# A fused encoder layer on Trainium2: residual rows folded into PSUM by identity products in the final stage

## The chip, the cores and the metric

The kernel is one program on one core of one Trainium2 chip. The metric is device time in microseconds for one execution, the median of several runs. All times inside the profile are microseconds from the start of the profiled execution's span.

## The reference, cut to what matters

One encoder layer over 1024 tokens of width 1024: RMSNorm, an input projection, three token mixers, an output projection with a residual add (its result is called `x1` in the kernel), then RMSNorm, a two-level router and a mixture of 32 experts of which each token uses two, a second residual add and a final RMSNorm.

```python
x = x + jnp.concatenate([o_a, o_b, o_c], axis=-1) @ w_out          # x1
x = x + hierarchical_moe(rmsnorm(x, norm2_g), ...)                  # two experts a token, each with its gate
...
return rmsnorm(x, final_g)                                          # x * rsqrt(mean(x*x) + eps) * final_g
```

What the final stage has to compute for each token is therefore: `s = x1 + gate0*y0 + gate1*y1`, where `y0` and `y1` are the output rows of its two experts, and then `s * rsqrt(mean(s*s) + 1e-6) * final_g`.

## The kernel before, in words

The stages run one after the other on one core: input projection, attention and pooling mixers, output projection, router, and then a loop over the 32 experts (from about 400 us to 806 us). In that loop every expert gathers its at most 80 rows from a table in HBM, TensorE multiplies them with the expert's weights, and the result rows are scattered by GpSimd's indirect DMA into the HBM tensor `expert_rows` (`y_d`): first choices in its rows 0 to 1023, second choices in rows 1024 to 2047. A branch for experts with more than 80 rows (`n_ovf > 0`) is in the program, and does no work on this input.

**The final stage**, which the change is about, works on 8 tiles of 128 tokens, `t = 0..7`; `x1[:, t, :]` (128 partitions x 1024 float32) already lies in SBUF.

- *SyncE* (lines 590 to 608) waits until all scatters have landed, and issues 16 loads of 512 KB each (`load_rows`, L596 and L597: `y0[t]`, then `y1[t]`, in the order of `t`), both on the semaphore `yc_in[t]`. After these it issues the 8 stores of the result (`store`, L601), each after a wait for `c_out`. All of them go into one hardware queue.
- *VectorE* makes, in the last expert's shadow, eight diagonal matrices `gdiag[i][k]` (L1627: the identity times the gate of each token). It then runs `add_rows(t)` and `finish(t)` in the order add 0, add 1, finish 0, add 2, finish 1 and so on to add 7, finish 6, finish 7.
- *TensorE* does a part of the sums. For the tiles in `PE_TILES = (1, 2, 4, 6)` it computes `gdiag0 @ y0 + gdiag1 @ y1` in two PSUM banks (L950, four float32 products of 128x128 by 128x512 a tile; the trace shows each as two records). `add_rows` of such a tile is one VectorE addition of PSUM and `x1` (L1650). For the other tiles (0, 3, 5, 7) `add_rows` is two multiply-adds from SBUF (L1655), no product.
- *ScalarE* takes the sum of squares of each finished sum (L1224) and adds eps (L1226), *GpSimd* raises it to the power -1/2 (L1848), and VectorE's `finish(t)` (L1661) multiplies the sum by that factor and by `final_g` into `fo[t]`. All three engines do this in the order of `t`.

The wait before TensorE's last-stage products is for both loads of a tile:

```python
for i, t in enumerate(PE_TILES):
    pe.wait_ge(diag_made, 2 * i + 2)
    pe.wait_ge(yc_in[t], 32)
```

Of the PSUM banks, `ps[0]` and `ps[1]` serve the expert loop's transposes, 2 and 3 its gate and up products, 4 to 7 its down products. The last expert's rows are copied out of banks 6 and 7 by ScalarE (L1207, counted in `y_out`) and VectorE (L1630, counted in `y_half`).

Of the kernel before, what the change touches and what calls it, by code (L numbers as in the profile page):

```python
# [24 lines left out]
ALU = mybir.AluOpType  # L25
ACT = mybir.ActivationFunctionType
# [6 lines left out]
P = 128  # L33
D = 1024
S = 1024
TT = S // P
# [26 lines left out]
POOL_LAG = 2  # L63
POOL_OPS = 16
PE_TILES = (1, 2, 4, 6)


ORDER = [4, 0, 5, 1, 11, 12, 13, 2, 3, 10, 6, 7, 8, 9]
# [41 lines left out]
def encoder(nc, x, norm1_g, w_in, nat_win, swa_sink, pool_w, pool_scale, w_out, norm2_g,  # L110
# [6 lines left out]
    y_d = nc.dram_tensor("expert_rows", [2 * S, D], F32).ap()  # L117

    with ExitStack() as ctx:
# [5 lines left out]
        def at(name, shape, dt, off):  # L125
            return nc.alloc_sbuf_tensor_at(name, shape, dt, offset=base + int(off))

        def sem(name):
            return ctx.enter_context(nc.semaphore(name))
# [3 lines left out]
        ident = at("ident", [P, P], F32, o); o += 512  # L133
        ones = at("ones", [P, P], F32, o); o += 512
        ut = at("ut", [P, P], F32, o); o += 512
        gbc = at("gbc", [P, D], F32, o); o += 4096
# [5 lines left out]
        stat = at("stat", [P, 4, TT], F32, o); o += 128  # L142
# [61 lines left out]
        x1 = at("x1", [P, TT, D], F32, TD)  # L204
# [42 lines left out]
        y0 = [at(f"y0{i}", [P, D], F32, H + 8192 * i) for i in range(TT)]  # L247
        y1 = [at(f"y1{i}", [P, D], F32, H + 8192 * i + 4096) for i in range(TT)]
        fo = [at(f"fo{i}", [P, D], F32, W + 4096 * i) for i in range(TT)]

        gdiag = [[at(f"gdiag{k}_{i}", [P, P], F32, W + 32 * KB + 512 * (2 * i + k)) for k in range(2)]
                 for i in range(len(PE_TILES))]

        ps = ctx.enter_context(nc.psum_tensor("ps", [P, 8, 512], F32))
# [107 lines left out]
        v_hT = sem("v_hT")  # L362
        v_ya = sem("v_ya")
        v_yv = sem("v_yv")
        yc_in = [sem(f"yc_in{i}") for i in range(TT)]
        c_sum = sem("c_sum")
        y_half = sem("y_half")
        diag_made = sem("diag_made")
        c_mm = sem("c_mm")
        c_eps = sem("c_eps")  # L370
        c_sq_done = sem("c_sq_done")
# [57 lines left out]

        def sums_done(t):  # L430

            return sum(1 if x in PE_TILES else 2 for x in range(t + 1))

        def raw_half(w, e, a):

# [20 lines left out]
        def _(sp):  # L456
# [136 lines left out]
            sp.wait_ge(y_put[0], n_ovf * 16 + 16 * (N_EXP // 2))  # L593

            def load_rows(t):
                sp.dma_start(y0[t][:], y_d[t * P:(t + 1) * P, :]).then_inc(yc_in[t], 16)  # L596
                sp.dma_start(y1[t][:], y_d[S + t * P:S + (t + 1) * P, :]).then_inc(yc_in[t], 16)  # L597

            def store(t):
                sp.wait_ge(c_out, t + 1)  # L600
# [2 lines left out]
            for t in range(TT):  # L603
                load_rows(t)
# [6 lines left out]
        def _(pe):  # L611
# [222 lines left out]
            def rows_transposed(src):  # L834

                for k in range(KT):
                    mm = nc.tensor.transpose(ps[:, k // 4, (k % 4) * COLS:(k % 4 + 1) * COLS],  # L837
                                             src[:, k * P:(k + 1) * P], ident[0:COLS, 0:COLS])
                return mm
# [71 lines left out]
            def v_gate_up(xTu):  # L911
                for f in range(4):
                    c0 = (f % 2) * P
                    for k in range(KT):
                        mm = nc.tensor.matmul(ps[:, 2, f * COLS:(f + 1) * COLS], wgu[0][:, f // 2, k, c0:c0 + P], xTu[:, k, :],
                                              start=(k == 0), stop=(k == KT - 1))
                return mm

            def v_down(hTu):
                for n in range(2):  # L920
                    for j in range(2):
                        mm = nc.tensor.matmul(ps[0:CAP, 4 + n, :], hTu[:, j, 0:CAP], wd[0][:, j, n * 512:(n + 1) * 512],
                                              start=(j == 0), stop=(j == 1))
                return mm
# [4 lines left out]
            with pe.If(n_ovf > 0):  # L929
                pe.wait_ge(v_hots, 1)  # L930
                for c in range(2 * TT):
                    mm = nc.tensor.matmul(ps[0:CAP, 3, 0:2 * N_OVF], ovf_row[:, c, :], ovf_tile[:, c].rearrange("p a j -> p (a j)"),
                                          start=(c == 0), stop=(c == 2 * TT - 1))
                mm.then_inc(v_list_mm, 1)
                with pe.Fori(0, N_OVF) as j:
                    with pe.If(j < n_ovf):
                        pe.wait_ge(v_x, j * 16 + 16)
                        rows_transposed(xg[0]).then_inc(v_tr, 1)
                        pe.wait_ge(v_xT, j + 1)
                        pe.wait_ge(v_w, j * 48 + 48)  # L940
                        v_gate_up(v_xTt).then_inc(v_gu, 1)
                        pe.wait_ge(v_hT, j + 1)
                        v_down(v_hTt).then_inc(down_done, 1)

            for i, t in enumerate(PE_TILES):
                pe.wait_ge(diag_made, 2 * i + 2)
                pe.wait_ge(yc_in[t], 32)
                for n in range(2):
                    for k, y in enumerate((y0[t], y1[t])):
                        mm = nc.tensor.matmul(ps[:, 2 * (i % 4) + n, :], gdiag[i][k][:], y[:, n * 512:(n + 1) * 512],  # L950
                                              start=(k == 0), stop=(k == 1))
                mm.then_inc(c_mm, 1)


        @block.scalar
        def _(act):
# [74 lines left out]
            def o_evacuate(s):  # L1031
                kind, i, g, _, _ = steps[s]
                oi = o_steps.index(s)
                act.wait_ge(pv_done, vnum[(s, last_chunk[s])] + 1)
                bank = ps[:, 6 + oi % 2, :]
                if kind == "na":
                    dst, src = oT[:, 0:2, i * P:(i + 1) * P], bank[:, 0:2 * P].rearrange("p (t q) -> p t q", t=2)
                else:
                    dst, src = oT[:, 2:6, i * P:(i + 1) * P], bank.rearrange("p (t q) -> p t q", t=4)
                nc.scalar.copy(dst, src).then_inc(o_out, 1)  # L1040
# [179 lines left out]
                        nc.scalar.copy(ysb[0][:, 0:512], ps[0:CAP, 4, :]).then_inc(v_ya, 1)  # L1220

            for t in range(TT):
                act.wait_ge(c_sum, sums_done(t))
                nc.scalar.activation(fo[t][:], x1[:, t, :], ACT.Square, scale=D ** -0.5, accum_out=stat[:, 0, t:t + 1]).then_inc(c_sq_done, 1)  # L1224
                act.wait_ge(c_sq_done, t + 1)
                nc.scalar.activation(stat[:, 1, t:t + 1], stat[:, 0, t:t + 1], ACT.Identity, bias=eps_col[:]).then_inc(c_eps, 1)  # L1226

# [2 lines left out]
        def _(dve):  # L1230
# [393 lines left out]
            dve.wait_ge(down_done, N_EXP - 1)  # L1624
            for i, t in enumerate(PE_TILES):
                for k in range(2):
# [16 lines left out]


            def add_rows(t):
                if t in PE_TILES:
                    i = PE_TILES.index(t)
                    dve.wait_ge(c_mm, i + 1)
                    b0 = 2 * (i % 4)
                    nc.vector.tensor_tensor(x1[:, t, :].rearrange("p (n d) -> p n d", n=2), ps[:, b0:b0 + 2, :],  # L1650
                                            x1[:, t, :].rearrange("p (n d) -> p n d", n=2), ALU.add).then_inc(c_sum, 1)
                    return
                dve.wait_ge(yc_in[t], 32)
                for k, y in enumerate((y0[t], y1[t])):
                    nc.vector.scalar_tensor_tensor(out=x1[:, t, :], in0=y[:], scalar=gates[:, k, t:t + 1], in1=x1[:, t, :],  # L1655
                                                   op0=ALU.mult, op1=ALU.add).then_inc(c_sum, 1)
                    dve.wait_ge(c_sum, sums_done(t) - 1 + k)

            def finish(t):
                dve.wait_ge(rstd_a, TT + t + 1)  # L1660
                nc.vector.scalar_tensor_tensor(out=fo[t][:], in0=x1[:, t, :], scalar=stat[:, 1, t:t + 1], in1=gbc[:],  # L1661
                                               op0=ALU.mult, op1=ALU.mult).then_inc(c_out, 1)

            dve.wait_ge(g_in, 48)
            add_rows(0)
            for t in range(TT):
                if t + 1 < TT:
                    add_rows(t + 1)
                finish(t)


        @block.gpsimd
# [238 lines left out]
```

## Time and profile before

| | us |
|---|---|
| median of 3 runs | 853.67 (852.27 to 855.41) |
| the profiled execution, its own time | 855.69 |
| span of that execution in the profile | 853.9 |
| TensorE busy | 749.4 (88%) |
| VectorE busy | 510.6 (60%) |
| ScalarE busy | 435.7 (51%) |
| GpSimd busy | 289.7 (34%) |
| last product of the expert loop ends | about 805.6 |
| from there to the end of the span | 48.3 |

The final stage is thus the last 5.7% of the span. The busy shares of the whole span say nothing of it: they are sums over stages with other limits. It has to be read from views that are limited to this stretch: the chain of waits, the timeline by engine, the landings of the DMAs and tables of windows. In a timeline row the columns are the start, the duration, engine, line, operation, tile written and tiles read, and in brackets the idle time of the engine before it with what ended it. PE is TensorE, PEld its weight loads, DVE VectorE, ACT ScalarE, POOL GpSimd, SPq SyncE's queue of DMA issues.

### The profile page before, as it was taken

How to read it: one execution, taken by the hardware profiler on the slowest of the kernel's cores; microseconds unless marked ns; L12 is line 12 of the kernel's file. 1: busy time of each engine (PE TensorE's matmuls, PEld its weight loads, DVE VectorE, ACT ScalarE, POOL GpSimd, SP SyncE). 2: the span in 40 equal slices, each digit the busy share in tenths (PEclk: the TensorE clock that was granted, in tenths of full speed). 3: DMA queues.
4: the chain of work that ended last, by engine and by line, in shares of the span. 5: the costliest groups of instructions: out<-in, count | busy, mean ns of one | idle time of the engine just before them, and what ended most of it. 6: DMA issues, size and time to landing. Idle time of an engine off the chain costs nothing.

```text
span 853.9 us, 10370 instructions
## 1 busy us (share of the span) xinstructions
PE 749.4 (88%) x3852; PEld 538.5 (63%) x3852; DVE 510.6 (60%) x776; ACT 435.7 (51%) x635; POOL 289.7 (34%) x240
## 2 busy tenths in 40 slices
PE   3899999999996888799899489999999999999761
PEld 2788888876664555488788456666666656656420
DVE  5551000016767888531357769888778888878547
ACT  6311112125555887700212278887777777778323
POOL 2533355615635767060101112222222233321111
PEclk9999999997999999999999589999999999999976
DMA  8362111100010000333463839999999999998195
GB/s 283 86 174 64 50 36 44 44 1 1 2 50 1 0 1 1 124 99 124 152 230 106 325 133 329 385 368 372 377 377 370 368 365 371 372 372 312 54 377 212
DMA packets 54947, 160.39 MB, mean 188 GB/s; under 512 B 9344, under 2 KB 24160, under 8 KB 46576
## 3 DMA queue, kind: packets, MB, share of 16 engines
q1 hardware_dynamic: 48352, 142.26, 46.1%
q0 software_dynamic: 6400, 16.92, 5.9%
q8 instruction: 32, 0.52, 0.2%
q10 hardware_dynamic: 144, 0.52, 0.2%
q14 instruction: 19, 0.16, 0.1%
HBM read 145.01 MB, written 18.87 MB: 192 GB/s over the span
## 4 chain that ended last, share of the span: by engine, by line
PE 60%; DMA 18%; DVE 10%; ACT 6%; issue 3%; SPq 1%; POOL 0%; POOLq 0%; ACTq 0%; DVEq 0%
DMA wgu<-in_expert_w_up 13%; PE ps L632 6%; PE ps L633 6%; PE ps L634 6%; PE ps L859 4%; PE ps L864 4%; PE ps L867 4%; PE ps L755 3%; PE ps L672 3%; PE ps L757 3%; PE ps L756 3%; PE ps L697 2%; DVE wgulo L1574 2%; PE ps L713 2%; PE ps L886 2%
## 5 line engine op out<-in xcount | busy, mean ns | idle before, releaser
L1574 DVE TENSOR_TENSOR wgulo<-wgu,unit 128x2048 fp32r<-128x2048 f32 x64 | 144.0, 2288 | 46.8 <-ACT unit L1137 46.8
L1137 ACT CAST unit<-wgu 128x2048 fp32r<-128x2048 f32 x64 | 120.3, 1909 | 33.1 <-DMA wgu<-in_expert_w_up 26.8
L1816 POOL DMA_INDIRECT expert_rows<-ysb,idx x32 | 51.8, 1618 | 169.4 <-ACT ysb L1184 160.1
L632 PE MATMUL ps<-hThi,whi 128*128 128x512 f32 x224 | 89.7, 400 | 4.2 <-DVE hTlo L1241 4.2
L633 PE MATMUL ps<-hTlo,whi 128*128 128x512 f32 x224 | 88.9, 397 | 0.0
L634 PE MATMUL ps<-hThi,wlo 128*128 128x512 f32 x224 | 88.7, 396 | 0.0
L1580 DVE TENSOR_TENSOR wdlo<-wd,unit 128x2048 fp32r<-128x2048 f32 x32 | 73.4, 2292 | 5.3 <-ACT unit L1146 5.3
L859 PE MATMUL ps<-unit,xThi 128*80 128x512 f32 x256 | 71.9, 402 | 0.0
L864 PE MATMUL ps<-unit,xTlo 128*80 128x512 f32 x256 | 70.0, 395 | 0.0
L867 PE MATMUL ps<-wgulo,xThi 128*80 128x512 f32 x256 | 69.8, 394 | 0.0
L1309 DVE CUSTOM_DVE_ANT_0 pna<-ps,te 128x512 f32<-128x512 f32 x16 | 10.9, 688 | 93.6 <-PE ps L672 93.4
L1771 POOL TENSOR_SCALAR pswa<-pswa,esum 128x384 f32<-128x384 f32 (+1 forms) x48 | 55.6, 1167 | 31.7 <-DVE esum L1329 31.2
L1809 POOL DMA_INDIRECT xg<-h_rows,idx x32 | 38.5, 1203 | 78.5 <-PE ps L837 63.7
L1146 ACT CAST unit<-wd 128x2048 fp32r<-128x2048 f32 x32 | 60.9, 1902 | 0.0
L755 PE MATMUL ps<-wohi,oThi 128*128 128x512 f32 x128 | 51.9, 405 | 4.0 <-DVE oTlo L1361 3.6
L864 PEld LDWEIGHTS ps<-unit,xTlo 128*80 128x80 f32 x256 | 38.2, 149 | 21.5 <-issue 0.7
L632 PEld LDWEIGHTS ps<-hThi,whi 128*128 128x128 f32 x224 | 43.0, 192 | 13.7 <-issue 4.7
L867 PEld LDWEIGHTS ps<-wgulo,xThi 128*80 128x80 f32 x256 | 38.2, 149 | 21.3 <-issue 0.7
L756 PE MATMUL ps<-wolo,oThi 128*128 128x512 f32 x128 | 50.1, 392 | 0.0
L757 PE MATMUL ps<-wohi,oTlo 128*128 128x512 f32 x128 | 50.1, 391 | 0.0
L1028 ACT ACTIVATE pswa<-pswa,mneg 128x385 f32<-128x385 f32 (+1 forms) x64 | 37.6, 589 | 22.5 <-DVE mneg L1322 22.1
L634 PEld LDWEIGHTS ps<-hThi,wlo 128*128 128x128 f32 x224 | 43.1, 193 | 9.3
(194 smaller groups left out, 1490.3 us busy)
## 6 DMA issues: line engine op xcount, KB each, us to landing
wgu<-in_expert_w_gate SPq DMA_DIRECT2D x32, 1024.0 KB, 17.4
wgu<-in_expert_w_up SPq DMA_DIRECT2D x32, 1024.0 KB, 21.9
wd<-in_expert_w_down SPq DMA_DIRECT2D x32, 1024.0 KB, 16.6
y<-expert_rows SPq DMA_DIRECT2D x16, 512.0 KB, 9.5
wraw<-in_w_in SPq DMA_DIRECT2D x14, 512.0 KB, 3.9
xin<-in_x SPq DMA_DIRECT2D x8, 512.0 KB, 5.6
xres<-in_x SPq DMA_DIRECT2D x16, 256.0 KB, 3.4
out<-fo SPq DMA_DIRECT2D x8, 512.0 KB, 2.6
```

Of the source, the lines that this page charges most:

```text
L632: nc.tensor.matmul(bank, whi[i % 2][:, k, :], hThi[:, k, cols], start=(k == 0), stop=False)
L633: nc.tensor.matmul(bank, whi[i % 2][:, k, :], hTlo[:, k, cols], start=False, stop=False)
L634: mm = nc.tensor.matmul(bank, wlo[i % 2][:, k, :], hThi[:, k, cols], start=False, stop=(k == KT - 1))
L755: nc.tensor.matmul(ps[:, g % 4, :], oThi[t][:, k, :], wohi[n][:, k, :], start=(k == 0), stop=False)
L756: nc.tensor.matmul(ps[:, g % 4, :], oThi[t][:, k, :], wolo[n][:, k, :], start=False, stop=False)
L757: mm = nc.tensor.matmul(ps[:, g % 4, :], oTlo[t][:, k, :], wohi[n][:, k, :], start=False, stop=(k == KT - 1))
L859: nc.tensor.matmul(bank, xThi[e % 2][:, 4 * a + k, :], hi[:, :, k * DE:(k + 1) * DE], start=(a == 0 and k == 0), stop=False)
L864: nc.tensor.matmul(bank, xTlo[e % 2][:, 4 * a + k, :], hi[:, :, k * DE:(k + 1) * DE], start=False, stop=False)
L867: mm = nc.tensor.matmul(bank, xThi[e % 2][:, 4 * a + k, :], lo[:, :, k * DE:(k + 1) * DE], start=False, stop=(a == 1 and k == 3))
L1137: nc.scalar.copy(weight_unit(e, a)[:], raw_half(wgu, e, a)).then_inc(ahi_done, 1)
L1574: nc.vector.tensor_tensor(raw_half(wgulo, e, a), raw_half(wgu, e, a), weight_unit(e, a)[:].bitcast(F32), ALU.subtract).then_inc(alo_done, 1)
L1580: nc.vector.tensor_tensor(wdlo[e % RING][:].rearrange("p j d -> p (j d)").rearrange("p (a f) -> p a f", a=2), wd[e % RING][:].rearrange("p ...
```

## The change

Nothing before the final stage changes. In it:

- TensorE first runs `FILL_LAST = 16` products of the identity with 128 columns of ones into bank 0, whose result is overwritten. It then puts the residual rows `x1[:, t, :]` of its four tiles into their banks by products with the identity (8 products of 128x128 by 128x512, `start=True`), before any row has landed. The expert rows are then accumulated on top (`start=False`), `y0` as soon as it is there and `y1` after it. Four tiles use all eight banks; the fourth waits for `y_half`, since VectorE copies the last expert's rows out of bank 7. 
- Inside the branch for overflow, which isn't taken here, TensorE gets two further waits.
- The addition in VectorE (L1650) is gone. For these four tiles ScalarE's sum of squares and VectorE's `finish` read PSUM directly (`sum_of(t)`), and ScalarE waits for TensorE's `c_mm` in place of VectorE's `c_sum`.
- Each load has a semaphore of its own (`yc_in[k][t]`), so that a multiply-add or product of `y0` does not wait for `y1`.
- VectorE's order is written out: add 0, finish 0, add 3, finish 1, 2, 3, add 5, finish 4, add 7, finish 5, 6, 7.

```diff
+FILL_LAST = 16
...
-        yc_in = [sem(f"yc_in{i}") for i in range(TT)]
+        yc_in = [[sem(f"yc_in{k}_{i}") for i in range(TT)] for k in range(2)]
...
         def sums_done(t):
 
-            return sum(1 if x in PE_TILES else 2 for x in range(t + 1))
+            return 2 * sum(x not in PE_TILES for x in range(t + 1))
+
+        def sum_of(t):
+
+            if t in PE_TILES:
+                i = PE_TILES.index(t)
+                return ps[:, 2 * i:2 * i + 2, :]
+            return x1[:, t, :].rearrange("p (n d) -> p n d", n=2)
...
             def load_rows(t):
-                sp.dma_start(y0[t][:], y_d[t * P:(t + 1) * P, :]).then_inc(yc_in[t], 16)
-                sp.dma_start(y1[t][:], y_d[S + t * P:S + (t + 1) * P, :]).then_inc(yc_in[t], 16)
+                sp.dma_start(y0[t][:], y_d[t * P:(t + 1) * P, :]).then_inc(yc_in[0][t], 16)
+                sp.dma_start(y1[t][:], y_d[S + t * P:S + (t + 1) * P, :]).then_inc(yc_in[1][t], 16)
...
                         v_down(v_hTt).then_inc(down_done, 1)
-
+                        pe.wait_ge(v_ya, j + 1)
+                        pe.wait_ge(v_yv, j + 1)
+
+            def last_rows(i, rows, weight, first, last):
+
+                for n in range(2):
+                    mm = nc.tensor.matmul(ps[:, 2 * i + n, :], weight[:], rows[:, n * 512:(n + 1) * 512], start=first, stop=last)
+                return mm
+
+            for _ in range(FILL_LAST):
+                nc.tensor.matmul(ps[:, 0, 0:P], ident[:], ones[:], start=True, stop=True)
             for i, t in enumerate(PE_TILES):
-                pe.wait_ge(diag_made, 2 * i + 2)
-                pe.wait_ge(yc_in[t], 32)
-                for n in range(2):
-                    for k, y in enumerate((y0[t], y1[t])):
-                        mm = nc.tensor.matmul(ps[:, 2 * (i % 4) + n, :], gdiag[i][k][:], y[:, n * 512:(n + 1) * 512],
-                                              start=(k == 0), stop=(k == 1))
-                mm.then_inc(c_mm, 1)
+                if i == 3:
+                    pe.wait_ge(y_half, 1)
+                last_rows(i, x1[:, t, :], ident, True, False)
+            pe.wait_ge(diag_made, 2 * len(PE_TILES))
+            for i, t in enumerate(PE_TILES):
+                pe.wait_ge(yc_in[0][t], 16)
+                last_rows(i, y0[t], gdiag[i][0], False, False)
+                pe.wait_ge(yc_in[1][t], 16)
+                last_rows(i, y1[t], gdiag[i][1], False, True).then_inc(c_mm, 1)
...
             for t in range(TT):
-                act.wait_ge(c_sum, sums_done(t))
-                nc.scalar.activation(fo[t][:], x1[:, t, :], ACT.Square, scale=D ** -0.5, accum_out=stat[:, 0, t:t + 1]).then_inc(c_sq_done, 1)
+                if t in PE_TILES:
+                    act.wait_ge(c_mm, PE_TILES.index(t) + 1)
+                else:
+                    act.wait_ge(c_sum, sums_done(t))
+                nc.scalar.activation(fo[t][:].rearrange("p (n d) -> p n d", n=2), sum_of(t), ACT.Square, scale=D ** -0.5,
+                                     accum_out=stat[:, 0, t:t + 1]).then_inc(c_sq_done, 1)
...
             def add_rows(t):
-                if t in PE_TILES:
-                    i = PE_TILES.index(t)
-                    dve.wait_ge(c_mm, i + 1)
-                    b0 = 2 * (i % 4)
-                    nc.vector.tensor_tensor(x1[:, t, :].rearrange("p (n d) -> p n d", n=2), ps[:, b0:b0 + 2, :],
-                                            x1[:, t, :].rearrange("p (n d) -> p n d", n=2), ALU.add).then_inc(c_sum, 1)
-                    return
-                dve.wait_ge(yc_in[t], 32)
+
                 for k, y in enumerate((y0[t], y1[t])):
+                    dve.wait_ge(yc_in[k][t], 16)
...
-                nc.vector.scalar_tensor_tensor(out=fo[t][:], in0=x1[:, t, :], scalar=stat[:, 1, t:t + 1], in1=gbc[:],
+                nc.vector.scalar_tensor_tensor(out=fo[t][:].rearrange("p (n d) -> p n d", n=2), in0=sum_of(t), scalar=stat[:, 1, t:t + 1],
+                                               in1=gbc[:].rearrange("p (n d) -> p n d", n=2),
                                                op0=ALU.mult, op1=ALU.mult).then_inc(c_out, 1)
...
             add_rows(0)
-            for t in range(TT):
-                if t + 1 < TT:
-                    add_rows(t + 1)
-                finish(t)
+            finish(0)
+            add_rows(3)
+            finish(1)
+            finish(2)
+            finish(3)
+            add_rows(5)
+            finish(4)
+            add_rows(7)
+            finish(5)
+            finish(6)
+            finish(7)
```

## Rows read from the trace of the kernel before

**Rows 1.** Chain that ended last, final stage: start, us, what.
```profile
807.14 3.73 DMA expert_rows<-ysb,idx
...
812.31 6.61 DMA y<-expert_rows
...
819.05 9.17 PE ps L950 x16
...
847.67 1.28 DVE fo L1661
```

**Rows 2.** Windows: stretch, length, busy PE, PEld, DVE, ACT, POOL, clock, DMA share, GB/s.
```profile
807.00:819.00 12.00, 0.00 (x0) 0.00 (x0) 2.57 (x2) 0.43 (x1) 0.91 (x1) 0.61 0.67 246
...
814.60:834.50 19.90, 15.23 (x30) 6.52 (x31) 11.18 (x10) 5.59 (x12) 2.33 (x3) 0.78 1.02 401
...
834.50:838.20 3.70, 1.02 (x3) 0.19 (x1) 3.67 (x4) 1.63 (x4) 1.53 (x2) 1.00 0.87 357
```

**Rows 3.** Timeline of VectorE in the final stage, three of its rows.
```profile
815.93 2.61 DVE L1655 SCALAR_TENSOR_TENSOR x<-y,gates,x 128x1024 f32<-128x1024 f32 x2 [9.64 <-DMA y<-expert_rows]
824.88 1.22 DVE L1650 TENSOR_TENSOR x<-ps,x 128x1024 f32<-128x1024 f32 x1 [6.34 <-PE ps L950]
...
842.90 2.60 DVE L1655 SCALAR_TENSOR_TENSOR x<-y,gates,x 128x1024 f32<-128x1024 f32 x2
```

**Rows 4.** Groups of instructions by line and shape: busy us, mean ns | idle before.
```profile
L1655 DVE SCALAR_TENSOR_TENSOR x<-y,gates,x 128x1024 f32<-128x1024 f32 x8 | 10.3, 1282 | 9.8 <-DMA y<-expert_rows 9.6
L1661 DVE SCALAR_TENSOR_TENSOR fo<-x,stat,gbc 128x1024 f32<-128x1024 f32 x8 | 10.2, 1280 | 1.0 <-POOL stat L1848 0.9
...
L1650 DVE TENSOR_TENSOR x<-ps,x 128x1024 f32<-128x1024 f32 x4 | 4.9, 1221 | 7.3 <-PE ps L950 7.3
```

**Rows 5.** SyncE's loads by line: issues, first and last start; then time to landing.
```profile
L596 SPq DMA_DIRECT2D y<-expert_rows x8: 335/443/870, 811.0 to 818.5; - x8
...
DMA to landing us min/median/max: 3.6/9.2/14.4
...
L597 SPq DMA_DIRECT2D y<-expert_rows x8: 432/441/894, 811.4 to 819.0; - x8
...
DMA to landing us min/median/max: 4.5/9.9/15.5
```

**Rows 6.** Stores 1, 3 and 8: issue, and under it its time to landing.
```profile
827.32 0.34 SPq L601 DMA_DIRECT2D out<-fo  x1
DMA to landing us min/median/max: 8.4/8.4/8.4
...
834.52 0.33 SPq L601 DMA_DIRECT2D out<-fo  x1
DMA to landing us min/median/max: 3.7/3.7/3.7
...
848.99 0.33 SPq L601 DMA_DIRECT2D out<-fo  x1
DMA to landing us min/median/max: 2.6/2.6/2.6
```

**Rows 7.** Timelines of ScalarE and GpSimd, the last two tiles.
```profile
845.53 1.06 ACT L1224 ACTIVATE fo<-x 128x1024 f32<-128x1024 f32 x1 [2.23 <-DVE x L1655]
...
843.38 1.21 POOL L1848 TENSOR_TENSOR stat<-stat,neg_half 128x1 f32<-128x1 f32 x1 [1.91 <-ACT stat L1226]
847.09 0.55 POOL L1848 TENSOR_TENSOR stat<-stat,neg_half 128x1 f32<-128x1 f32 x1 [2.50 <-ACT stat L1226]
```

**Rows 8.** TensorE: two weight loads of the timeline, then two windows as in rows 2.
```profile
821.74 0.34 PEld L950 LDWEIGHTS ps<-y,gdiag 128*128 128x128 f32 x1 [0.52 <-issue]
...
824.18 0.19 PEld L950 LDWEIGHTS ps<-y,gdiag 128*128 128x128 f32 x1 [0.24 <-issue]
...
809.50:810.00 0.50, 0.00 (x0) 0.00 (x0) 0.00 (x0) 0.00 (x0) 0.00 (x0) 0.53 0.47 148
...
823.20:823.40 0.20, 0.20 (x2) 0.08 (x1) 0.00 (x0) 0.00 (x0) 0.00 (x0) 1.00 1.04 430
```

## The prediction

> **What bounds the kernel now.** I read the chain of waits first, since busy shares of the whole span tell nothing of its last 48 us. There [rows 1] the final stage is a sequence: the last scatter, the loads of the expert rows, 9.2 us of TensorE's products for tiles 1 and 2, and from 828.2 to the end VectorE almost alone. The last `finish` starts at 847.67, its store is issued at 848.99 and lands 2.6 us later [rows 6], at 851.6; the span ends 2.3 us behind it, at 853.9. I keep this tail of 2.3.
>
> The windows [rows 2] then show what stands idle. TensorE does nothing from 807 to 819. The DMA engines are full from 814.6 to 834.5 at 401 GB/s. VectorE's timeline [rows 3] has a hole of 6.34 us before the addition of tile 1, which waits for products; after it VectorE has little idle time up to the last tile.
>
> Third, the landings [rows 5]. Issue plus time to landing gives 814.6 for the first `y0`, 815.9 for the first `y1`, 832.9 for the last `y0` and 834.5 for the last `y1`: 19.9 us for 15 steps, 1.33 a load; 401 GB/s is 1.31 for 524,288 bytes. I looked up all 16; from the fourth (818.9) to the fifteenth (832.9) they are 1.27 apart. The first store, issued at 827.32, landed at 835.7, and the third, issued at 834.52, at 838.2 [rows 6]. A store thus queued behind the loads, and the loads kept their pace; from the last load on, three stores landed in 3.7 us, 1.23 each. I take 1.28 for a transfer in a full queue.
>
> Last, TensorE's clock. It worked until 805.6, and the granted clock fell to half (1.2 GHz) in the window from 809.5 to 810; with work from 819.05 it was full (2.4 GHz) from 823.2 [rows 8]. Weight loads of the record pairs stand 0.85 us apart at half clock and 0.43 at full (the row behind each one shown is at 822.60 and at 824.61). A product of 512 columns, two records, costs 1.71 or 0.86; a tile's four cost 6.8 or 3.4.
>
> **The change part by part.**
>
> *The addition goes.* Four additions at 1.22 [rows 4] leave VectorE: 4.9 us. For its `finish` from PSUM there is no row. The nearest is the addition itself, with one operand in PSUM: 1.221, against 1.280 for `finish` from SBUF [rows 4]. I take 1.25; bounds 1.19 and 1.35, so at most 0.4 over the four.
> The Trainium skill speaks against this (page "VectorE: DVE Perf Modes", section on the TRN2 errata): a VectorE pass has a fixed cost of 58 cycles from SBUF and 120 from PSUM, an estimate of 0.065 us more for each pass, 0.26 for four. The rows of the addition show no such surcharge, and the sum below has room for it.
>
> *Fills and identity products.* TensorE can begin when the last copies out of its banks end, at 806.3 (two waits that already stand before the branch); I take 806.9, when GpSimd's queue came through its own branch. 16 fills are 32 records: at least a quarter of 0.43 each (3.4 us), at most a weight load of 0.19 each (6.1). The eight products cost 8 x 0.86 = 6.9. They end between 817.2 and 819.9. Until 817.6, when the first row for TensorE lands, nothing else wants the engine: that idle time is the cover. `y_half` came at 806.3, so its wait is free. If the first instruction after the branch comes late, the end moves by as much.
>
> *Expert rows.* Without backlog, `y0` of tile 1 is done at 819.3, `y1` at 821.0, tile 2 at 824.4. With products ending at 819.9 it is 826.8. Tile 4 is done 1.7 after its `y1` (826.6): 828.3. Tile 6: 831.7 + 1.7 = 833.4. The longest pause is 2.1 us, shorter than that from 805.6 to 809.5 through which the clock stayed full, so I take full clock throughout.
>
> *One semaphore a row.* Tiles 0, 3, 5 and 7 can begin 1.3 us earlier. It is worth 1.3 only where VectorE waits for a load: tile 3, and at the end tile 7. The number of DMAs and their order in the queue stay; no queue is passed.
>
> *VectorE's new order*, with 2.14 us from a finished sum to its factor if none waits in line (845.50 to 847.64 for tile 7; tile 6's power step took 1.21 and not 0.55 beside a multiply-add, which makes it 2.8) [rows 7]. A pair of multiply-adds is 2.6 [rows 3].
> Add 0 ends at 818.5, as now; finish 0 at 822.0. Add 3: its `y1` lands at 824.1, end 825.4. Finish 1: 826.6. Finish 2: sum at 824.4, factor 826.6, end 827.8. Finish 3: ScalarE comes from tile 2 at 825.9, factor 828.1, end 829.4. Add 5 (landed at 829.2): 832.0. Finish 4: 833.2. Add 7: first half 834.5, second after the landing at 834.5, end 835.8. Finish 5 and 6: 838.3. Factor 7: 835.8 + 2.14 to 3.3, which is 837.9 to 839.1; finish 7 ends by 840.4. Now it is 848.95: VectorE gives back 8.5 us.
> The cost of writing the order out: add 5 and add 7 stand behind finish 2 and 3. If tile 2's products are late, all that follows is late, the multiply-adds with it.
>
> *What is late next.* A lone store issued at 840.4 would land at 843.0. But it isn't alone. Stores 1 to 5 are issued by 833.3, before the loads are through, and the sixth at 837.1. The queue stays full, and the last landing is set by it: 838.2 for the third store, as today, plus five at 1.28 is 844.6 (bounds 1.23 and 1.33: 844.3 and 844.9). VectorE has 1.6 us to spare. The span ends at 844.6 + 2.3 = 846.9, **7.0 us less**. Of 8.5 us that VectorE gives back, 1.5 are lost in the queue.
>
> The profiled execution took 855.69 (span 853.9), 2.0 above the median of 853.67. Taken from the median, 7.0 gives **846.7**.
>
> **The rivals.**
>
> *A: TensorE late by its own extra work.* Each us by which tile 2 is done after 826.0 (824.4 + 1.6) moves the end. With fills at 0.19 it is 826.8, cost 0.8; with a start 2 us later as well, 2.8. Time 847.5 to 849.5. For it: nothing in the trace shows the branch's exit on TensorE, or fills. Against: the mean of the fill bounds leaves no cost.
>
> *B: stores take turns with the loads.* Then four stores issued before 829.5 push the last `y1` from 834.5 to 839.6. Add 7 ends at 840.9, finish 7 by 844.3 (3.4 later, as now), end of span 844.3 + 2.6 + 2.3 = 849.2; time 849.0. Against: store 1 needed 8.4 us and landed a step behind the last load [rows 6]. For: that load's step was 1.6, not 1.27.
>
> *C: stores alone run slower than loads.* The stretch in which three landed moved 357 GB/s [rows 2], 1.47 us a store: 834.5 + 8 x 1.47 + 2.3 = 848.6, time 848.4. That window holds idle time too, so I give it little.
> The Trainium skill (page "DMA: Bandwidth & Descriptors", section "Where 436 GB/s comes from") says that for HBM transfers the HBM side binds, near 358 GB/s, which comes to the same; the 401 GB/s of the loads is above it, and the measurement decides.
>
> *D, slower: TensorE at half clock.* If fills and products kept the granted clock at half, the eight identity products cost 13.7 and the fills at least 6.8: end at 827.4. Sixteen expert products at 1.71 are 27.4, all in line: tile 6 at 854.8. Then 2.1 for its factor, finish 6 and 7 (2.5), store and tail (4.9): 864.3, time 864.1. It decides once tile 6 is done after 844.4 (848.95 - 2.1 - 2.5), against 833.4 forecast. Against: the clock rose under just these products within 4.2 us [rows 8], and they begin with it still full.
>
> *E: the addition was not what held the end*, another wait takes its place, and the time stays within 2 us of now. VectorE was busy nearly all the last 20 us, which speaks against it.
>
> **How the numbers follow.** Forecast 0.62, A 0.16, B 0.07, C 0.04, E 0.07, D 0.04. A measurement of this kernel can tell about 0.5% (4.3 us) from no change: faster means below 849.4. The forecast, C and most of A and B lie there: 0.84; E and the rests of A and B are "same", 0.12; D is slower, 0.04. The range takes the forecast down by 1.8 (0.3 for a quicker queue, 1.5 for the spread of the runs, 852.27 to 855.41) and up to 850.4, A and B with 1 us of spread: 844.9 to 850.4.
>
> **What would show it.** L1650 is absent, `finish` of tiles 1, 2, 4, 6 reads PSUM in 1.19 to 1.35. TensorE runs from 807 to between 817 and 820 at full clock, and c_mm 1 and 2 come near 821 and 824.5. The last load lands near 834.5, the stores 1.28 apart with no gap up to 844.6, the last one more than 2.6 after its issue. I am wrong if that store needs just 2.6 (VectorE or TensorE is then the bound, A), if loads are late (B), or if the granted clock is 0.5 behind 823 (D).

## The result, and the profile after

| | before | after |
|---|---|---|
| median of 5 runs | 852.75 (851.58 to 855.41) | 845.28 (844.45 to 846.41) |
| the profiled execution, its own time | 855.69 | 846.11 |
| its span | 853.9 | 844.3 |
| issue of the last scatter | 807.14 | 806.48 |
| from there to the landing of the last load | 27.4 | 27.3 |
| to the issue of the last store | 41.8 | 32.4 |
| to its landing | 44.5 | 37.4 |
| to the end of the span | 46.7 | 37.8 |

The ratio of after to before is 0.9887, with an interval of 0.9867 to 0.9908: 9.6 us less of 852.75 (7.8 to 11.3). The medians of the five runs of each are only 7.5 apart (a ratio of 0.9912, just outside that interval; where the difference comes from is open), the two spans 9.6. The change is faster, as forecast. By how much more than the forecast's 7.0 us depends on which of these is taken: by the ratio, from the 853.67 that the forecast started from, the time is 844.0, below the lower end of 844.9; by the medians alone it would be close to the forecast. The profiles settle what the end of the kernel gained and where, and there the forecast missed a part.

The last four rows of the table tell where. I count from the last scatter there and in the experiments, since what lies ahead of the final stage, which the change doesn't touch, moved by up to 5.4 us between my runs of all kernels (its issue was between 804.6 and 810.0). From the scatter to the last landing it is 7.1 us less (44.5 to 37.4), and the forecast said 7.0. Then 0.66 us lie ahead of the scatter. The rest, 1.8 us, is in the tail, the stretch from the landing of the last store to the end of the span: 2.2 us before, 0.4 after. I had kept it fixed.

The windows of the changed kernel (columns as in [rows 2]), where the first is TensorE's new work, the second the stretch from the first to the last load, the third most of the stores:

```profile
806.10:816.80 10.70, 10.69 (x48) 6.54 (x49) 2.57 (x2) 0.03 (x1) 0.91 (x1) 1.00 0.61 219
814.00:833.90 19.90, 17.32 (x39) 6.78 (x37) 15.24 (x13) 9.10 (x19) 4.88 (x6) 1.00 1.02 400
833.90:841.50 7.60, 0.00 (x0) 0.00 (x0) 4.96 (x4) 2.21 (x6) 1.62 (x3) 0.67 1.03 420
```

TensorE is busy where it was idle in [rows 2], at the full granted clock, and the clock stays full through the loads (0.78 in the mean before). The DMA engines are full (1.02 and 1.03) from the first load to the last stores. TensorE's timeline gives the fills (L962), the identity products and the expert products of tiles 1 and 2, 4 and 6 (L958):

```profile
806.11 3.84 PE L962 MATMUL ps<-ones,ident 128*128 128x128 f32 x32 [1.20 <-ACT ysb L1227]
809.78 7.03 PE L958 MATMUL ps<-x,ident 128*128 128x512 f32 x16
816.82 7.11 PE L958 MATMUL ps<-y,gdiag 128*128 128x512 f32 x16
824.40 3.70 PE L958 MATMUL ps<-y,gdiag 128*128 128x512 f32 x8 [0.47 <-DMA y<-expert_rows]
829.52 3.70 PE L958 MATMUL ps<-y,gdiag 128*128 128x512 f32 x8 [1.42 <-DMA y<-expert_rows]
```

The work ahead of the rows ends at 816.8, just as the first row for TensorE lands (816.7). VectorE's timeline, of which [rows 3] were the rows before:

```profile
814.13 2.61 DVE L1673 SCALAR_TENSOR_TENSOR x<-y,gates,x 128x1024 f32<-128x1024 f32 x2 [8.51 <-DMA y<-expert_rows]
...
824.49 1.28 DVE L1679 SCALAR_TENSOR_TENSOR fo<-ps,stat,gbc 128x1024 f32<-128x1024 f32 x1
826.06 1.28 DVE L1679 SCALAR_TENSOR_TENSOR fo<-ps,stat,gbc 128x1024 f32<-128x1024 f32 x1 [0.29 <-POOL stat L1874]
...
833.90 1.28 DVE L1673 SCALAR_TENSOR_TENSOR x<-y,gates,x 128x1024 f32<-128x1024 f32 x1 [0.16 <-DMA y<-expert_rows]
...
837.62 1.28 DVE L1679 SCALAR_TENSOR_TENSOR fo<-x,stat,gbc 128x1024 f32<-128x1024 f32 x1
```

The last finish begins at 837.62, 10 us earlier than in [rows 1]. The groups by line and shape set the new `finish` from PSUM beside the one from SBUF:

```profile
L1679 DVE SCALAR_TENSOR_TENSOR fo<-x,stat,gbc 128x1024 f32<-128x1024 f32 x4 | 5.1, 1283 | 2.4 <-POOL stat L1874 2.3
L1679 DVE SCALAR_TENSOR_TENSOR fo<-ps,stat,gbc 128x1024 f32<-128x1024 f32 x4 | 5.1, 1282 | 0.4 <-POOL stat L1874 0.3
```

They cost the same, 1.28. The last two stores in SyncE's timeline, and their time to landing (by source line, in the window from 838):

```profile
837.73 1.52 SPq L609 DMA_DIRECT2D out<-fo  x2
...
DMA to landing us min/median/max: 4.9/4.9/4.9
```

4.9 us, not the 2.6 of a store by itself [rows 6]: the queue is still full. Counted from the scatter, the eight stores of the changed kernel landed at 28.7, 29.9, 31.1, 32.4, 33.6, 34.9, 36.2 and 37.4, 1.25 apart, though they were issued with gaps of up to 5.5 us between them. This is the forecast's mechanism, and its sum (844.6, which is 37.5 behind the scatter's 807.14) is 0.1 off.

**The tail.** At the end of the kernel every engine runs a closing DRAIN instruction, which in the trace ends behind the engine's last work, and then meets the others at a barrier. The instructions of the source line of that barrier, of the kernel before (count, least/median/longest ns, first and last start us):

```profile
L119 POOLq EVENT_SEMAPHORE  x2: 17/17/17, 853.7 to 853.7; - x2
...
L119 POOLq DRAIN  x1: 6567/6567/6567, 847.1 to 847.1; - x1
...
L119 SPq COMPARE_BRANCH  x1: 38/38/38, 851.6 to 851.6; - x1
```

and of the changed kernel:

```profile
L120 POOLq EVENT_SEMAPHORE  x2: 17/17/17, 844.1 to 844.2; - x2
...
L120 POOLq DRAIN  x1: 6564/6564/6564, 836.7 to 836.7; - x1
...
L120 SPq COMPARE_BRANCH  x1: 38/38/38, 843.9 to 843.9; - x1
```

SyncE passes its wait for the last store at 851.6 before, but GpSimd's drain began with its last power step at 847.1, took 6.57 us, and so ended at 853.6; the barrier opened at 853.7. In the changed kernel the drain ended at 843.3 and SyncE came at 844.0. So before, the end was held by GpSimd's last instruction and its drain; afterwards by the last store. The chain of waits says hardly anything of it: it ends at the last `finish`, and all that it has of the drain is this step ahead of it:

```profile
847.05 0.60 POOLq L119
```

The waits of SyncE put those 2 us down to another engine's queue:

```profile
SPq L119 <- PEq L119: 2.0, 1, 2.0
```

TensorE's drain had ended at 835.6. The experiments test this reading.

### The profile page after: what moved, and what is told of

It reads as the page before. It is cut to its first block, busy times and chain, and to the rows that moved or that the text cites. A ratio compares the mean times of both kernels' runs of the same rounds, so it can differ in the third digit from the quotient of the medians.

```text
span 844.3 us, 10463 instructions
## 1 busy us (share of the span) xinstructions
PE 757.2 (90%) x3900; PEld 544.0 (64%) x3900; DVE 505.8 (60%) x772; ACT 435.2 (52%) x635; POOL 284.7 (34%) x240
## 4 chain that ended last, share of the span: by engine, by line
PE 59%; DMA 19%; DVE 9%; ACT 6%; issue 3%; SPq 2%; DVEq 0%; POOL 0%; POOLq 0%; ACTq 0%
DMA wgu<-in_expert_w_up 13%; PE ps L640 6%; PE ps L641 6%; PE ps L642 6%; PE ps L867 4%; PE ps L872 4%; PE ps L875 4%; PE ps L763 3%; PE ps L765 3%; PE ps L764 3%; PE ps L705 2%; DVE wgulo L1598 2%; PE ps L680 2%; PE ps L721 2%; PE ps L894 2%
## 5 line engine op out<-in xcount | busy, mean ns | idle before, releaser
L1835 POOL DMA_INDIRECT xg<-h_rows,idx x32 | 37.8, 1182 | 81.1 <-PE ps L845 65.3
L872 PEld LDWEIGHTS ps<-unit,xTlo 128*80 128x80 f32 x256 | 38.3, 150 | 21.8 <-issue 1.2
L875 PEld LDWEIGHTS ps<-wgulo,xThi 128*80 128x80 f32 x256 | 37.8, 148 | 21.0
L1048 ACT ACTIVATE pswa<-pswa,mneg 128x385 f32<-128x385 f32 (+1 forms) x64 | 37.7, 589 | 22.4 <-DVE mneg L1346 22.1
```

The source lines that it names most:

```text
L872: nc.tensor.matmul(bank, xTlo[e % 2][:, 4 * a + k, :], hi[:, :, k * DE:(k + 1) * DE], start=False, stop=False)
L875: mm = nc.tensor.matmul(bank, xThi[e % 2][:, 4 * a + k, :], lo[:, :, k * DE:(k + 1) * DE], start=False, stop=(a == 1 and k == 3))
```

## The experiments

All times are from the issue of the last scatter, in one profiled execution each. Of the experiments only b_nopow7 was run ten times; the whole times of the others are single ones, from 847.57 (a_again) to 853.72 (a_nofold), and carry what lies ahead of the scatter too, so I do not compare them. "Held by" names which came last at the barrier, SyncE behind the last store or GpSimd's drain.

| run | last load landed | last store issued | landed | end | held by |
|---|---|---|---|---|---|
| kernel before | 27.4 | 41.8 | 44.5 | 46.7 | drain |
| b_nopow7 | 27.5 | 41.4 | 44.0 | 44.4 | store |
| b_sems | 27.1 | 40.9 | 43.5 | 45.7 | drain |
| a_nofold | 27.1 | 38.2 | 40.8 | 43.1 | drain |
| a_oldorder | 27.5 | 35.7 | 38.3 | 40.6 | drain |
| a_nofill | 27.5 | 36.2 | 39.0 | 40.8 | drain |
| changed kernel | 27.3 | 32.4 | 37.4 | 37.8 | store |
| a_again | 27.9 | 33.0 | 37.9 | 38.3 | store |
| a_nopow7 | 28.2 | 33.3 | 38.2 | 38.6 | store |
| a_late_pool | 27.8 | 33.4 | 37.7 | 40.2 | drain |
| a_delay1 | 27.5 | 33.9 | 37.4 | 37.9 | store |
| a_delay2 | 27.5 | 35.1 | 38.7 | 39.1 | store |
| a_actstore | 32.4 | 37.5 | 40.3 | 42.1 | drain |

**Was the tail the drain? b_nopow7.**

```diff
-            for t in range(TT):
+            for t in range(TT - 1):
                 pool.wait_ge(c_eps, t + 1)
                 gp.tensor_tensor(stat[:, 1, t:t + 1], stat[:, 1, t:t + 1], neg_half[:], ALU.pow).then_inc(rstd_a, 1)
...
-                dve.wait_ge(rstd_a, TT + t + 1)
+                if t < TT - 1:
+                    dve.wait_ge(rstd_a, TT + t + 1)
+                else:
+                    dve.wait_ge(c_eps, TT)
```

> The kernel before, with one step left out: GpSimd's power of -1/2 for tile 7; VectorE multiplies tile 7 by mean square plus eps in its place. Everything is counted from the issue of the last scatter, since what lies ahead of it moves by up to 0.7 us from run to run (kernel before: 46.7 to the end of the span). Theory, drain: GpSimd's closing drain of 6.57 us, which begins when it takes its last power step, held the end of the kernel before, and not the last store. Now its last step is that of tile 6, begun 3.7 us earlier; the drain ends some 2.4 to 3.1 us earlier, before the last store has landed, finish 7 comes some 0.6 earlier, and the tail from SyncE's last landing to the end of the span shrinks from 2.2 to 0.4: 44.2 to 44.5 from the last scatter, time about 2.4 us less. Rival, a fixed tail behind the last store (of TensorE's sequencer, which the view of waits names): 0.6 less alone, tail still 2.2.

Measured 44.4, 2.3 less, and a ratio of 0.9976 (0.9952 to 1.0001) to the kernel before, about the 0.28% that 2.4 us are, though the interval just touches no change. Its closing instructions:

```profile
L119 POOLq DRAIN  x1: 7219/7219/7219, 844.3 to 844.3; - x1
...
L119 SPq COMPARE_BRANCH  x1: 38/38/38, 851.9 to 851.9; - x1
```

The drain now covers all of the power step of tile 6 (1.20 us in place of 0.55, so 7.22) and ended at 851.5, ahead of SyncE; the tail is 0.4. Of the 2.3 us, 0.5 are the earlier landing of the last store (44.0 for 44.5) and 1.8 the tail. The fixed tail is refuted.

**The same on the changed kernel, a_nopow7** (the same edit).

> The changed kernel with the same step left out (GpSimd's power for tile 7; VectorE multiplies tile 7 by mean square plus eps). Theory: the queue of stores holds the end, the drain ended 0.7 us before it already, and finish 7 was not waiting for its factor; 37.8 us from the last scatter to the end, as in the changed kernel, within 0.3, tail 0.4. Rival, the drain holds the end here too: about 1.5 to 2 us less.

38.6: no gain, the tail again 0.4. It came out 0.8 above the first run of the changed kernel and so outside the 0.3 that I had allowed; its last two loads took 1.8 and 1.6 instead of 1.3, and its last store 2.0. How far that repeats is seen in a_again, below.

**A late step on GpSimd, a_late_pool.**

```diff
+            pool.wait_ge(c_out, TT)
+            gp.tensor_tensor(stat[:, 0, 0:1], stat[:, 1, 0:1], neg_half[:], ALU.pow).then_inc(rstd_a, 1)
```

> The changed kernel with one more power step of 128x1 on GpSimd after the last finish has ended (839.0 in the changed kernel's profile); nobody waits for its result. Theory, drain: the drain begins there and ends 6.57 us later, at 845.6, so the span ends 1.6 us later (39.4 from the last scatter, the tail behind the last landing 2.0). Rival, fixed tail or queue alone: no change (37.8), as the step ends 4 us before the last landing.

```profile
L120 POOLq DRAIN  x1: 6564/6564/6564, 840.7 to 840.7; - x1
...
L120 SPq COMPARE_BRANCH  x1: 37/37/37, 845.0 to 845.0; - x1
```

The drain ends at 847.2, the barrier opens there, and the tail behind the last landing is 2.5. The end is at 40.2 and not 39.4, since this run's last `finish` came at 33.4 and not 32.5 from the scatter; from that point the reckoning holds to 0.1. A step that nobody waits for costs 1.9 us against a_again (2.4 against the changed kernel's first profile): the drain is a cost of the last GpSimd instruction, wherever it stands.

**How much time has VectorE to spare? a_delay2 and a_delay1.**

```diff
             finish(6)
+            for s7 in (7, 5):
+                nc.vector.scalar_tensor_tensor(out=y1[s7][:], in0=y0[7][:], scalar=gates[:, 0, 7:8], in1=gbc[:], op0=ALU.mult, op1=ALU.mult)
             finish(7)
```

> The changed kernel with two more passes of 128x1024 on VectorE (1.2 us each, into rows that nobody reads any more) between finish 6 and finish 7. Theory, the queue of 24 transfers holds the end: the last store is issued 2.4 us later, at about 841.3 for 838.9, and still lands with the queue at 843.9; the span stays within 0.3 of 37.8 from the last scatter, time from issue to landing of the last store falls from 4.9 to 2.6. Rival, VectorE holds the end: 2.4 us later.

Neither: 39.1, about 1.1 above the mean of the changed kernel's two runs for a delay of 2.4. The last store was issued at 842.83, 35.1 from the scatter, and took 3.6 us to land, where I had expected the 2.6 of a lone one. It wasn't held up by the store ahead of it, which landed at 36.3. Two windows behind its issue, and under them the same two behind the issue of the lone last store of the kernel before (848.99):

```profile
842.80:843.60 0.80, 0.00 (x0) 0.00 (x0) 0.01 (x1) 0.00 (x0) 0.00 (x0) 0.50 0.13 51
843.60:845.00 1.40, 0.00 (x0) 0.00 (x0) 0.00 (x0) 0.00 (x0) 0.00 (x0) 0.50 0.93 375
```
```profile
849.00:849.80 0.80, 0.00 (x0) 0.00 (x0) 0.00 (x0) 0.00 (x0) 0.00 (x0) 0.50 0.01 0
849.80:851.20 1.40, 0.00 (x0) 0.00 (x0) 0.00 (x0) 0.00 (x0) 0.00 (x0) 0.50 0.92 375
```

Both began to move 0.8 us after their issue and had moved 1.4 later, so in a_delay2 the queue had run dry and VectorE held the end. The 1.0 us more lies between the last bytes and the landing (1.4 in place of 0.4), and why is open. The second run, with one pass in place of two (`s7 in (7,)`), and the kernel itself again:

> The changed kernel with one more pass of 1.2 us on VectorE before finish 7. Two such passes cost 1.3 us and the last store then took 3.6 us from issue to landing behind another one, not the 2.6 of a lone store. Theory, the queue holds the end up to a last issue at 33.8 us from the last scatter (37.4 - 3.6): one pass moves the issue from 32.4 to 33.7, costs nothing, and the last store lands within 0.3 of the other landings' pace: same end as a_again within 0.4. Rival, VectorE holds the end: 1.2 later.

> The changed kernel once more, to see how far its times from the last scatter repeat: 37.8 to 38.6 to the end of the span, as the one run of it and its twin without tile 7's power gave, with the last landing set by the queue.

a_delay1 ended at 37.9, a_again at 38.3: one pass of 1.2 us is free. The last store of a_delay1:

```profile
843.17 0.33 SPq L609 DMA_DIRECT2D out<-fo  x1
```

landed 3.6 us later, 37.4 from the scatter. Together with a_delay2, VectorE's time to spare is between 1.2 us and 2.4. An estimate from a_delay2: its DMA engines stopped being full at 842.2 and were all but idle by 843.0, and a store begins to move 0.8 behind its issue, so an issue at 33.7 to 34.5 from the scatter would just have kept them busy, 1.3 to 2.1 later than the 32.4 of the changed kernel; the forecast had 1.6. The changed kernel repeats within 0.5 us.

**What each part is worth: a_oldorder, a_nofold, b_sems, a_nofill.** First VectorE's order as before:

```diff
             add_rows(0)
-            finish(0)
-            add_rows(3)
...
-            finish(7)
+            for t in range(TT):
+                if t + 1 < TT and t + 1 not in PE_TILES:
+                    add_rows(t + 1)
+                finish(t)
```

> The changed kernel with VectorE's order of before (add t+1 unless TensorE has the sum, then finish t: add 0, finish 0 and 1, add 3, finish 2 and 3, add 5, finish 4 and 5, add 7, finish 6 and 7). From the last scatter to the end of the span; changed kernel 37.8. Theory: add 7 stands behind finish 5, ends some 3 us later than in the changed kernel, and two ends follow it: GpSimd's last power step and its drain of 6.57 us, to 39.9, and the last store, to about 39. So 39.9, set by the drain. Rival, the order is worth nothing because the queue of 24 transfers holds the end: 37.8 to 38.2.

40.6, held by the drain (from 839.6 to 846.2, with SyncE at 844.3). VectorE's timeline shows the price of the order:

```profile
834.25 1.28 DVE L1679 SCALAR_TENSOR_TENSOR fo<-x,stat,gbc 128x1024 f32<-128x1024 f32 x1 [0.85 <-POOL stat L1867]
835.46 2.60 DVE L1673 SCALAR_TENSOR_TENSOR x<-y,gates,x 128x1024 f32<-128x1024 f32 x2
```

The last pair begins 29.6 us from the scatter, 3.6 later than in the changed kernel, behind `finish(5)`, which waits 0.85 for its factor. Its last store landed at 38.3, so without the drain the end would be 38.7, by reckoning: of the 2.8 us that the order is worth, 1.9 come through GpSimd's drain.

Then, on top of that, the residual in VectorE again:

```diff
-                last_rows(i, y0[t], gdiag[i][0], False, False)
+                last_rows(i, y0[t], gdiag[i][0], True, False)
...
+            def add_product(t):
+                i = PE_TILES.index(t)
+                dve.wait_ge(c_mm, i + 1)
+                nc.vector.tensor_tensor(x1[:, t, :].rearrange("p (n d) -> p n d", n=2), ps[:, 2 * i:2 * i + 2, :],
+                                        x1[:, t, :].rearrange("p (n d) -> p n d", n=2), ALU.add).then_inc(c_add, 1)
...
+            for t in range(TT):
+                if t + 1 < TT:
+                    (add_product if t + 1 in PE_TILES else add_rows)(t + 1)
+                finish(t)
```

> The same as a_oldorder, and besides the residual is added by VectorE again (four passes of 1.2 us as in the kernel before; TensorE runs the same fills and identity products, but the first product of the expert rows overwrites them). From the last scatter: theory, VectorE's four additions stand in its chain ahead of the last pair of multiply-adds, which ends 3.2 us later than in a_oldorder; with the drain behind it 43.1, against 46.7 of the kernel before, whose remaining 3.6 us are the half clock and the joint wait of TensorE's first products. Rival, folding is worth its full 4.9 us against a_oldorder: 44.8. Rival, the additions fill idle time: as a_oldorder.

43.1. Four additions of 1.2 us cost 2.5 us and not 4.9. The remainder filled idle time: in a_oldorder VectorE waits 3.19 us for the factor of tile 1, and 0.37 to 0.85 for those of four later tiles.

The semaphores alone, on the kernel before:

```diff
-                pe.wait_ge(yc_in[t], 32)
-                for n in range(2):
-                    for k, y in enumerate((y0[t], y1[t])):
+                for k, y in enumerate((y0[t], y1[t])):
+                    pe.wait_ge(yc_in[k][t], 16)
+                    for n in range(2):
```

> The kernel before with a semaphore of its own for each load, and TensorE's products of a tile in the order y0, y0, y1, y1. From the last scatter; kernel before 46.7. Theory: TensorE begins tile 1 when its y0 lands, 1.3 us earlier, its clock rises 1.3 earlier, and all that follows on VectorE and GpSimd with it: 45.4. Rival, the second product waits all the same and the clock rises no earlier: 46.7.

45.7, 1.0 less. TensorE's timeline, and two windows around the rise of its clock:

```profile
814.89 16.68 PE L950 MATMUL ps<-y,gdiag 128*128 128x512 f32 x32 [11.86 <-DMA y<-expert_rows]
```
```profile
820.00:820.30 0.30, 0.30 (x2) 0.16 (x1) 0.00 (x0) 0.00 (x0) 0.00 (x0) 0.50 1.01 410
820.60:820.90 0.30, 0.30 (x2) 0.19 (x1) 0.00 (x0) 0.00 (x0) 0.00 (x0) 1.00 1.07 437
```

TensorE began at 10.3 us from the scatter in place of 11.9, 1.6 earlier. The clock did not rise 1.3 earlier with it, as my theory had it: it was full from about 15.8 from the scatter, against 16.0 before, after 5.5 us of work at half clock in place of 4.2. The 1.0 comes from the earlier start at half clock; the first addition of a product in VectorE began at 16.8 from the scatter in place of 17.7.

And the changed kernel with `FILL_LAST = 0`:

> The changed kernel with no fills (16 products of 128 columns less; the identity products stay and end at about 6.5 us from the last scatter, 3.7 us before the first expert row for TensorE lands). From the last scatter; changed kernel 37.8. Theory: the granted clock falls to half at about 10.5 us, when the expert products begin, and is back 4 us later; tiles 1 and 2 come up to 2 us later, the multiply-adds behind finish 2 and 3 some 1.5 later, GpSimd's drain ends at 38.6. So 38.2 to 38.6. Rival, the clock stays full and the fills are worth nothing: 37.8.

40.8, where I expected at most 38.6. TensorE's timeline and two windows, the first from the fall of the clock to its rise:

```profile
808.48 7.13 PE L958 MATMUL ps<-x,ident 128*128 128x512 f32 x16 [1.21 <-ACT ysb L1227]
820.00 17.02 PE L958 MATMUL ps<-y,gdiag 128*128 128x512 f32 x32 [4.39 <-DMA y<-expert_rows]
```
```profile
819.40:826.00 6.60, 6.00 (x7) 2.52 (x8) 2.29 (x2) 1.05 (x3) 0.57 (x1) 0.50 1.02 411
826.20:832.00 5.80, 5.80 (x15) 2.59 (x14) 2.64 (x3) 3.18 (x7) 0.84 (x2) 1.00 1.03 415
```

The identity products ended at 815.6, TensorE stood for 4.4 us, the clock was at half (1.2 GHz) from 819.3, just before the first expert product, until 826.1, and seven records took 6 us that take 3 at full. That is 3 us; the first row for TensorE had also landed 0.8 later than in the changed kernel (11.0 and 10.2 from the scatter). The factor of tile 2 came 3.9 us later (finish 2 began at 23.4 and not 19.6), and finish 2, behind which add 5 and add 7 stand in the written order, passed it on: this is rival A's path. The end is 2.5 to 3.0 us later than in the two profiles of the changed kernel; the fills, 16 small products in idle time, are worth that less up to 0.8 for the later landing, which isn't shown to be their doing.

**Stores on a queue of their own, a_actstore.**

```diff
-            for t in range(TT):
+            for t in range(4, TT):
                 store(t)
...
+                if 1 <= t <= 4:
+                    act.wait_ge(c_out, t)
+                    act.dma_start(out[0, (t - 1) * P:t * P, :], fo[t - 1][:]).then_inc(out_put, 16)
```

> The changed kernel with stores 1 to 4 issued by ScalarE on its own queue, each after its square of the next tile. From the last scatter. Theory, turns: two queues share the DMA engines, so each of these four transfers delays the loads behind it by up to 1.3 us; the last load lands at up to 32.4 in place of 27.3, add 7 ends 5 us later, GpSimd's drain holds the end at up to 42.1. Rival, the engines serve transfers in the order of their issue whatever the queue: loads land as before and the end stays at 37.8 to 38.6.

42.1, as the theory of turns had it, to the tenth. The rival, service in the order of issue, is out: the first of these stores, issued at 822.2, 3.7 us behind the last load, landed 9 us ahead of it. The four stores, by source line, and their time to landing:

```profile
L1253 ACTq DMA_DIRECT2D out<-fo x4: 338/338/384, 822.2 to 830.2; - x4
...
DMA to landing us min/median/max: 6.9/7.6/8.1
```

They landed 6.9 to 8.1 us after their issue, in place of 10.1 to 14.8, and the last load landed 5.1 us later, at 32.4. Packets of both queues moved side by side: from 829 to 833 us, 1.00 MB in the queue of the loads and 0.69 in ScalarE's. All stores of the changed kernel stand in one queue behind the loads, and it is this which keeps early stores from costing anything.

I tried no version meant to beat the changed kernel. The runs point to no cheap one: by this count 24 transfers of 512 KB at 1.25 to 1.3 us each, the first of which lands 7.5 us behind the last scatter, end between 36.3 and 37.4 whatever the engines do; less would need fewer bytes or loads that start before the last scatter has landed. Neither was tried.

## Why the prediction was wrong, and where it was right

- *What holds the end: wrong.* The step that failed is the first: "the span ends 2.3 us behind it ... I keep this tail of 2.3". It is no constant but what GpSimd's drain had left over; b_nopow7 took it from 2.2 to 0.4, a_late_pool brought it back to 2.5. The tail before was a term of the sum that should have read 0.4 after; with it, the sum is 7.0 + 1.9 = 8.9 us, and 844.8 for the time. That is still 0.8 above the 844.0 of the ratio. The two profiles differ by 0.66 ahead of the last scatter, in a stretch that moved by up to 5.4 us between runs; what moves it, no run here shows. The rows were there to ask about: [rows 7] have GpSimd's last step at 847.09, and a tail of 2.3 behind SyncE's last landing had no owner in the text.
- *The queue: right.* The last landing was forecast at 37.5 from the scatter and measured at 37.4, with stores 1.25 apart and the last one 4.9 behind its issue. Rivals B and C are out in this kernel (last load at 27.3, as before; 420 GB/s through the stores); a_actstore shows that B's mechanism is real once a second queue is used.
- *Rival C's second ground.* The Trainium skill (page "DMA: Bandwidth & Descriptors", section "Where 436 GB/s comes from") has the HBM side bind near 358 GB/s. The windows above moved 400 (loads) and 420 (stores); no run here was held to 358.
- *TensorE's own work: right, cheaper than taken.* 32 fill records in 3.7 us (bounds 3.4 and 6.1), products in 7.0 (6.9), start at 806.1 (806.9). Tiles 1 and 2 were done at 14.0 and 17.4 from the scatter, forecast 13.9 and 17.3. Rival D's clock did not occur, but a_nofill shows its beginning: without the fills the clock does fall, for 6.8 us.
- *`finish` from PSUM: right, at 1.282 for 1.25.* By the Trainium skill (page "VectorE: DVE Perf Modes", section on the TRN2 errata) it would be an estimated 0.065 us above the one from SBUF; it is 0.001 below.
- *VectorE's gain: right in sum, smaller in its parts than I said.* 9.4 us earlier issue of the last store (forecast 8.5). "The addition goes: 4.9 us" was worth 2.5 at the end (a_nofold against a_oldorder). The order alone, to which the forecast gave no share of its own and of which it named only the risk, gave 2.8.
- *The division of the 8.9 us from the scatter* is, taking the parts away one on top of the other: 3.6 for TensorE ready and warm with a semaphore a row (46.7 to 43.1, of which 1.0 are the semaphores), 2.5 for the fold (to 40.6), 2.8 for the order (to 37.8). These single executions carry up to 0.5 us of scatter each.

## What to carry to other kernels

Before a tail is kept as a constant, find its owner: list the closing instructions of all engines, not only of the one that waits last. A GpSimd instruction, however small, that comes late in a kernel holds the end until its drain is over, here 6.6 us from the start of that instruction; take GpSimd out of the last steps, or see that something else ends later anyway. And where one hardware queue is full to the end, speeding up the engines ahead of it pays only down to the queue; count its transfers first.

## What the runs showed of the hardware that I had not expected

- GpSimd's closing drain took 6.56 to 6.57 us in all eleven runs in which its last step took 0.55, and 7.20 and 7.22 in the two in which that step took 1.18 and 1.20. In all thirteen it thus ended 6.0 us behind the end of the last step. The other engines' took 0.01 to 4.0.
- A lone store of 512 KB landed 2.6 us after its issue: 0.8 until it moved, 1.4 moving, 0.4 to the landing. In a_delay2 the last 0.4 was 1.4, so 3.6 in all, and the last store of a_delay1 took 3.6 too; the cause is open.
- Two hardware queues share the DMA engines: four early stores of 512 KB on a second queue delayed the last load by 5.1 us, 1.27 each (a_actstore); in the same queue they delayed it by nothing.
- The granted clock was at half for 6.8 us in a_nofill, with TensorE at work for 6.1 of them; before it rose TensorE had worked for 4.2 us in the kernel before [rows 8] and for 5.5 in b_sems.
